# Loading a recurrent state early into a retired key buffer, with two homes instead of three for the first value sets

## The reference, cut to what matters

```python
# group A, 4 heads: retention, starting from the stored state
ret_o, s_s = retention_chunked(rq, rk, rv, state_ret[layer], chunk_s)
# group B, 8 heads: attention over 2048 past tokens in pages
k_past = ck[pages].reshape(past_len, MOBA_HEADS, MOBA_HD)
v_past = cv[pages].reshape(past_len, MOBA_HEADS, MOBA_HD)
moba_o = moba_attend_seq(q, concat(k_past, kn), concat(v_past, vn), pos_s)
# then w_out, residual, and 32 experts, top 4 of them for each token
hres = x + mix @ w_out
y = hres + moe(rmsnorm(hres), ...)   # w_gate_up 1024x2048, w_down 1024x1024 for each expert
```

## Time and profile before

| | |
|---|---|
| median of 3 runs | 1220.76 us (1220.1 to 1220.95) |
| the profiled execution's own time | 1219.89 us |
| its span in the trace | 1218.1 us |
| tensor engine busy | 1183.0 us (97%) |
| vector / scalar / GpSimd busy | 382.8 / 237.8 / 68.1 us |
| moved by DMA | 500.65 MB, 411 GB/s over the span |
| granted clock of the tensor engine, mean | 0.999 |

### The profile page before, as it was taken

The page is one execution under the profiler, slowest core; times in us unless marked ns, Lnnn a source line. Parts: engine busy times, 40 slices in busy tenths (PEclk is TensorE's granted clock), DMA queues, the critical chain, the costliest instruction groups (busy, mean ns, idle before and its releaser), DMA issues.

```text
span 1218.1 us, 17287 instructions
## 1 busy us (share of the span) xinstructions
PE 1183.0 (97%) x7276; PEld 506.0 (42%) x7276; DVE 382.8 (31%) x541; ACT 237.8 (20%) x561; POOL 68.1 (6%) x70
## 2 busy tenths in 40 slices
PE   8999999999999999999999999999999999999996
PEld 5555545445343443434343434434343434343432
DVE  5999984534112112111111121221111111111123
ACT  3211263423011112112010102121111111110112
POOL 3222112320000000000000000000000000000000
PEclk9999999999999999999999999999999999999999
DMA  9999999999999999999999999999999999999995
GB/s 355 408 390 389 373 358 383 397 398 352 412 430 429 425 428 430 429 428 427 429 429 429 426 429 429 430 426 428 428 430 428 427 429 429 430 426 428 428 429 232
DMA packets 50283, 500.65 MB, mean 411 GB/s; under 512 B 5704, under 2 KB 6368, under 8 KB 19392
## 3 DMA queue, kind: packets, MB, share of 16 engines
q1 hardware_dynamic: 42672, 430.54, 84.5%
q0 software_dynamic: 7520, 69.47, 14.2%
q10 hardware_dynamic: 48, 0.01, 0.0%
HBM read 495.29 MB, written 4.72 MB: 410 GB/s over the span
## 4 chain that ended last, share of the span: by engine, by line
PE 64%; DMA 23%; DVE 7%; issue 4%; ACT 1%; SPq 0%; DVEq 0%; POOLq 0%
PE psum L1061 24%; DMA arena<-w_gate_up 18%; PE psum L1092 14%; PE psum L953 6%; DVE arena L1656 6%; DMA arena<-w_down 3%; PE psum L973 3%; PE psum L959 2%; PE psum L642 2%; PE psum L985 2%; PE psum L771 2%; PE psum L992 1%; DMA arena<-w_in 1%; PE psum L550 1%; PE psum L469 1%
## 5 line engine op out<-in xcount | busy, mean ns | idle before, releaser
L1061 PE MATMUL psum<-arena 128*64 128x512 f32 x1920 | 421.7, 594 | 11.6 <-DMA arena<-w_gate_up 11.5
L1061 PEld LDWEIGHTS psum<-arena 128*64 128x64 f32 x1920 | 135.0, 137 | 294.7 <-issue 267.8
L2004 DVE TENSOR_SCALAR arena<-psum 128x512 f32<-128x512 f32 x32 | 22.2, 692 | 674.7 <-PE psum L1061 635.8
L1092 PE MATMUL psum<-arena 128*64 128x512 f32 x960 | 212.6, 595 | 0.0
L1238 ACT ACTIVATE arena<-psum 64x512 f32<-64x512 f32 (+6 forms) x193 | 97.8, 510 | 383.6 <-PE psum L1092 170.6
L1656 DVE STREAM_TRANSPOSE arena<-arena 128x2048 f32<-128x2048 f32 x32 | 121.3, 3922 | 1.5 <-DMA arena<-cache_k,arena 1.4
L1092 PEld LDWEIGHTS psum<-arena 128*64 128x64 f32 x960 | 66.2, 136 | 124.3 <-issue 122.5
L550 PE MATMUL psum<-arena 128*128 128x512 f32 x224 | 103.2, 604 | 1.3 <-ACT arena L1238 0.7
L1513 ACT ACTIVATE arena<-arena 128x512 f32<-128x512 f32 x30 | 18.9, 631 | 412.4 <-DVE arena L2004 412.4
L953 PE MATMUL psum<-arena 128*128 128x128 f32 x512 | 76.8, 293 | 0.2 <-DVE arena L1916 0.2
L953 PEld LDWEIGHTS psum<-arena 128*128 128x128 f32 x512 | 66.4, 199 | 16.7 <-issue 12.7
(11 more groups left out here) (261 smaller groups left out, 695.6 us busy)
## 6 DMA issues: line engine op xcount, KB each, us to landing
arena<-w_gate_up SPq DMA_DIRECT2D x128, 2048.0 KB, 31.0
arena<-w_down SPq DMA_DIRECT2D x62, 2048.0 KB, 32.6
arena<-w_in SPq DMA_DIRECT2D x6, 2048.0 KB, 25.2
arena<-w_out SPq DMA_DIRECT2D x2, 2048.0 KB, 13.8
arena<-w_down SPq DMA_DIRECT2D x3, 1024.0 KB, 37.3
arena<-w_in SPq DMA_DIRECT2D x2, 1024.0 KB, 9.1
out<-arena POOLq DMA_DIRECT2D x1, 2048.0 KB, 20.5
out<-arena SPq DMA_DIRECT2D x3, 512.0 KB, 6.5
```

Source lines behind the costliest of these rows:

```text
L1061: last = mm(psum[64 * g:64 * (g + 1), b, :], xt[:, 2 * kk + m, lhs], gate_slot[slot][:, m, c:c + 512], start=False, stop=kk == 3 and m == ...
L1092: last = mm(psum[64 * g:64 * (g + 1), 2, :], at_sb[:, m, SLOTS * q:SLOTS * (q + 1)], down_slot[slot][:, m, 512 * g:512 * (g + 1)], start=q ...
```

## The change

The state is loaded as soon as the last key unit is scored (`k_scored` 32), ahead of blocks 7 and 8 in the sync engine's list. Its home, words 12288 to 16383, is no longer used by values. Value sets 0 to 5 alternate between the two homes at `KV`; from set 6 on there are three homes, `win` slot 0 among them for sets 6, 9, 12 and 15. So sets 2 to 5 each wait until the set two before them is used (`v_used` n - 1), set 6 waits for set 3 and for block 6 (`block6` is the mark after `sample_part(6)`), and sets 7 on wait as before, for the set three before. `PLACE` is turned so that expert loads 0, 1 and 2 still take the homes of sets 13, 14 and 15.

```diff
@@ -45,7 +45,7 @@
-PLACE = (7, 0, 6, 4, 5, 3, 1, 2)
+PLACE = (6, 7, 0, 4, 5, 3, 1, 2)
@@ -232,7 +232,7 @@
         def v_raw(n):
-            home = KV + 4096 * (n % 3) if n % 3 < 2 else 12288 if n < 6 else 0
+            home = KV + 4096 * (n % 2) if n < 6 else KV + 4096 * (n % 3 - 1) if n % 3 else 0
             return at(home, 8, 512)
@@ -2163,11 +2163,9 @@
                 if n < 2:
                     pool.wait_ge(k_trans, K_UNITS - 2 + 2 * n)
-                elif n == 2:
-                    pool.wait_ge(k_scored, K_UNITS)
                 else:
-                    pool.wait_ge(v_used, n - 2)
-                if n == 8:
+                    pool.wait_ge(v_used, n - 1 if n < 6 else n - 2)
+                if n == 6:
                     pool.wait_ge(*mark["block6"])
@@ -2259,11 +2257,11 @@
             load_block(6)
+            sp.wait_ge(k_scored, K_UNITS)
+            sp.dma_start(state.rearrange("p s h v -> p (s h) v"),
+                         t["state_ret"][0].rearrange("s h k v -> k (s h) v")).then_inc(state_in, 16)
             load_block(7)
             load_block(8)
-            sp.wait_ge(v_used, 6)
-            sp.dma_start(state.rearrange("p s h v -> p (s h) v"),
-                         t["state_ret"][0].rearrange("s h k v -> k (s h) v")).then_inc(state_in, 16)
```

## The result

The changed kernel takes 1236.47 us (median of 5 runs, 1233.83 to 1238.59) against 1220.95 us (5 runs): the ratio is 1.013, 95% interval 1.0119 to 1.014, so it is slower by 15.5 us. The prediction holds in sign and stated range (1232, 1226 to 1238). The value is 4.5 us above its central number and lies on its rival "Two clock falls" (likely 1236).

What follows compares the result with a forecast made beforehand. The tensor engine's pace in the head was taken to time the weight stream and so the end. 1219.9 + 10.7 (waits) - 0.7 (given back) + 2.0 (clock) = 1231.9, given as 1232 us, range 1226 to 1238.

Steps and rivals of the forecast that it cites:

- Two clock falls: Rival: both long waits, at sets 2 and 6, drop the clock, 2.0 to 4.6 us each; likely 1236 us; chance 0.20.
- One sign of being wrong: After the new waits in the head: the clock staying below full for longer than a few microseconds.
- What bounds the kernel: The tensor engine paces the head and so times the weight stream; a microsecond lost there moves the end by one.
- The waits: Tensor engine waits for value sets 2, 4 and 6 of 5.1, 0.6 and 4.9 us, making set 6 10.7 us late.
- the other queue: At set 2's fetch: the rest of block 8, in another queue, slows it by 2.0 us (bounds 0 and 3).
- Given back: Short waits for the scalar and vector engine in the head shrink by 0.7 us (bounds 0 and 1.5).
- The state's margin: In the kernel before, the state landed at 216.5 and its reader starts at 218.97, so nobody waited for it.
- The clock: At the new waits in the head: one fall to half speed, costing 2.0 us (bounds 0 and 4.6).
- Faster fetches: Rival: value fetches land some 2.5 us sooner, set 2 isn't slowed; +3 to +5 us, 1224 us; chance 0.07.
- Waits hidden by the loop's slack: Rival: the expert loop waits for weights anyway, so the head's delay vanishes; 1220 us; chance 0.04.
- Faster by filling the DMA engines' hole: Rival: the early state fills the hole at 162 to 168 us, gaining up to 2.3 us; 1217.6 us; chance 0.04.
- The state's price on the path: Moving the state's load from 189.74 frees 7.6 us of DMA engine time there, but buys nothing on the path.

Runs made afterwards that it cites:

- the change's second execution: The unaltered change run and traced again, used because the first trace had set 0 about 2.1 us late: 1236.07 us, ratio 1.0127.
- experiment 7: The change plus spare matmuls before the waits for sets 2 and 6; three tries: 1245.58, 1239.98 and, with exactly 256 more instructions, 1231.09 us.
- Experiment 6: The change with blocks 7 and 8 loaded only after set 3 is used: 1232.57 us, ratio 1.0097.
- experiment 2: The change's two homes, but the state and blocks 7 and 8 loaded in the order of the kernel before: 1240.71 us, ratio 1.0158.
- experiment 4: The kernel before, with set 6's fetch also waiting for block 6: 1238.8 us, ratio 1.0144.
- experiment 3: The kernel before, with set 2's fetch also waiting until set 0 is used: 1226.64 us, ratio 1.0053.
- experiment 1: The kernel before with the state loaded early, sets 2 and 5 in win slot 1 and block 7 after set 5: 1220.11 us, ratio 0.9993.

## Why the prediction was right, and what was off

The mechanism was right, the number only in part. The central 1232 is 4.5 us too low, and the forecast's own range of 1227 to 1236 misses the median of 1236.47. The stated range holds it only because its upper end was stretched to take in the middle of the rival "Two clock falls". One sign of being wrong came true too: the clock stayed below full for longer than a few microseconds.

The starts below come from the timelines of before, of the change's second execution and of the third try in experiment 7 (us):

| | before | change | clock kept |
|---|---|---|---|
| set 0 | 160.94 | 160.98 | 161.14 |
| set 2 | 169.41 | 174.60 | 174.66 |
| set 3 | 174.92 | 182.62 | 181.62 |
| set 6 | 192.32 | 205.16 | 203.72 |
| set 7 | 197.24 | 212.65 | 208.64 |
| first weight load | 241.34 | 256.75 | 252.72 |
| loop's first weight matmul (L1061) | 296.73 | 313.70 | 309.57 |
| end of the span | 1218.1 | 1234.8 | 1231.5 |

The rows of the change behind the middle column:

```profile
174.60 3.65 PE L642 MATMUL psum<-arena 128*32 128x512 f32 x16 [5.09 <-DMA arena<-cache_v,arena]
...
182.62 1.95 PE L642 MATMUL psum<-arena 128*32 128x512 f32 x16
...
205.16 3.65 PE L642 MATMUL psum<-arena 128*32 128x512 f32 x16 [4.80 <-DMA arena<-cache_v,arena]
212.65 1.95 PE L642 MATMUL psum<-arena 128*32 128x512 f32 x16
...
256.75 0.35 SPq L2273 DMA_DIRECT2D arena<-w_gate_up  x1
```

**What bounds the kernel: right.** The loop starts 17.0 us later and the span ends 16.7 us later. The delay of the head goes to the end almost whole.

**The waits: right in their places and sizes, in part by luck.** Set 2 landed 10.8 us after its issue, as summed (8.8 and 2.0). Experiment 6 shows that the other queue was the right cause, but with the blocks gone set 2 lands in 8.1, so the terms were rather 8.1 and 2.7, and two errors of 0.7 us cancelled. The waits of 5.1, 0.6 and 4.9 us were 5.09, 0.19 and 4.80. The one at set 4 shrank since the slow clock behind set 2 held the tensor engine back while the fetch went on. The reckoned landing of set 3 at 179.4 was too early: with the clock kept, the tensor engine waits for it until 181.62, where in the change the slow clock hides its lateness.

```profile
174.66 1.95 PE L649 MATMUL psum<-arena 128*32 128x512 f32 x16 [0.35 <-DMA arena<-cache_v,arena]
...
181.62 1.95 PE L649 MATMUL psum<-arena 128*32 128x512 f32 x16 [1.38 <-DMA arena<-cache_v,arena]
```

**Given back: wrong, nothing was.** From set 7 to the first weight load both kernels take 44.10 us. The short waits for the scalar and vector engine move with the tensor engine.

**The state's margin: misread.** The prediction set the landing at 216.5 against L807 at 218.97. The tensor engine's wait for the state stands one step earlier, before L803 at 218.62, so the margin was 2.1 us and not 2.5. This changed nothing in the sum, but the margin mattered in experiments 2 and 4.

**The clock: the step that was mis-sized.** I took one fall of 2.0 us. There were two on the path, and experiment 7 prices them at 5.0 us together by the medians, 4.2 us by the traces. In the table: from set 2 to set 3 the change takes 8.02 us instead of 5.51 (2.5 lost), and from set 6 to set 7 7.49 instead of 4.92 (2.6 lost). Against the clock-kept run the fall at set 2 is worth less, 1.6 us up to set 6 (44.18 against 42.58 us from set 0), mainly since a wait for set 3 of 1.4 us would stand in its place; the one at set 6 keeps its 2.6. Half speed lasts some 7 us, of which 1.2 to 1.6 us fall into the wait itself. The rival "Two clock falls" had the price (4.0 to 9.2) and the time (1236).
The Trainium skill, "TensorE: Matmul & The Clock Gate", part 1, was the better guide here: an idle engine is dropped to half rate and has to be busy for a while to come back, and by it both waits counted. The traces agree, with a granted clock of 0.50 to 0.51 behind both. My argument that 5 us was hardly longer than the 4.1 us at the end of the trace was weak, and experiment 3 refutes it: there the clock fell after 2.5 us idle. It need not: after 2.85 us at set 6 of experiment 6 it did not fall, and the third fall below came without a wait, so idleness alone does not tell when it falls.

**A third fall, not foreseen.** From the first weight load to the loop the change takes 56.95 us instead of 55.39, with the fall at 268 to 272 in it: 1.6 us. It was there in both executions of the change and at 264 to 268 with the clock kept, but also in the traces of experiments 1 and 3 (at 256 to 260), so whether the change makes it likelier is open.

The sum of the change's parts, stretch by stretch against before: waits 10.1, falls at sets 2 and 6 5.1, third fall 1.6, together 16.8, against 16.7 in the spans. The medians are 15.1 to 15.5 us apart. A likely reason, not tested, is that the runs of before contain falls too: the nine beside experiment 7 have mean clocks of 0.996 to 0.998, the traced execution 0.999.

**The other rivals.** Faster fetches: no, 8.1 to 9.1 us alone in the queue. Waits hidden by the loop's slack: no, experiment 3. Faster by filling the DMA engines' hole: not here, as set 2 landed 10.8 us after its issue and not in 5.7; experiment 1 moved the hole rather than closed it. **The state's price on the path: missed.** I wrote that its move buys nothing, which holds with three homes (experiment 1). With two homes it isn't so: left in its old place it would have cost another 5.6 us.

No variant beats the kernel before. Experiment 1's comes out the same; of those with two homes, the lowest median is that of the one with the clock kept.

## What to carry to other kernels

Price a buffer taken from a rotation by the round trip: use, fetch issued, landed. Here two homes left 8 to 11 us of fetch behind 5.5 us of work, and the clock added a third to two thirds to such a wait (1.6 on 5.1, 2.6 on 4.8, 1.7 on 2.5). Before a transfer is moved out of an engine's way, look at what shares the queues at its new place and at how thin the margin of its reader is at the old one: 2.1 us of margin was spent by a wait elsewhere. And when experiments add instructions ahead of a loop, watch the instruction loads; they can cost more than what is measured.

## What the runs showed of the hardware

- A wait of the tensor engine of 2.51 us was followed by half the granted clock (experiment 3), one of 2.85 us was not (experiment 6, set 6). The clock also fell near 156 us and at 256 to 271 us, in stretches without any wait over 1 us, in some executions and not in others, at about 3.0 us and 1.4 to 1.6 us each.
- With 39 or 79 more instructions ahead of the loop there were 69 instruction loads instead of 32, and the tensor engine waited 1.8 to 2.4 us at each of the loop's four turns back; with 256 more there were 34 and no such wait.
- A 2 MB load in 512-byte pieces took 26.8 us to land with value fetches issued at 190.44, 195.11, 200.03 and 210.47 beside it (before), and 42.2 us with three issued within 2.6 us around its own issue (experiment 2).
